# First unit's transposes of probabilities two ticks behind their row instead of one, in a three-branch decoder trunk on one core

## The reference

```
h = rmsnorm(x, norm_g[i]);  proj = h @ w_in[i]
ya = forgetting_attention(qa, ka, va, logf) * silu(za)        # 8 heads of 64, causal, forget-gate bias
yb = nsa_attention(...compressed, selected, window...) * silu(zb)
yc = differential_attention(qc, kc, vc, lam, ...) * silu(zc)  # 4 heads, two maps each
merged = g0*(ya @ w_br_a) + g1*(yb @ w_br_b) + g2*(yc @ w_br_c)
x = x + merged @ w_out[i]
x = x + sigmoid(x @ w_ple_gate[i]) * (p[i] @ w_ple[i])
```

## Time and profile before

| | us |
|---|---|
| median of 3 runs | 1517.42 |
| lowest and highest run | 1516.68, 1519.68 |
| the profiled execution, its own time | 1517.52 |
| its span from the first to the last instruction | 1515.7 |
| TensorE busy | 1476.7 (97%) |
| VectorE busy | 938.1 (62%) |
| ScalarE busy | 634.6 (42%) |
| mean granted clock of TensorE | 0.996 |

### The profile page before, as it was taken

The page is one execution under the profiler, slowest core; times in us unless marked ns, Lnnn a source line. Parts: engine busy times, 40 slices in busy tenths (PEclk is TensorE's granted clock), DMA queues, the critical chain, the costliest instruction groups (busy, mean ns, idle before and its releaser), DMA issues.

```text
span 1515.7 us, 22245 instructions
## 1 busy us (share of the span) xinstructions
PE 1476.7 (97%) x7765; PEld 1225.4 (81%) x7765; DVE 938.1 (62%) x2197; ACT 634.6 (42%) x1499; POOL 75.6 (5%) x79
## 2 busy tenths in 40 slices
PE   7999999999999999999999999999999999999997
PEld 6778778888888887888787887888888888878885
DVE  6866765655557776454576667655556567855544
ACT  6543434434344344343444434334434444434343
POOL 1000000000001000000100000000000000000011
PEclk9999999999999999999999999999999999999998
DMA  7334443223335543332342335423324355433322
GB/s 195 90 82 121 104 112 77 70 70 77 83 93 139 139 119 84 109 102 70 108 110 70 105 99 126 115 54 82 77 63 118 88 131 130 108 102 100 87 87 74
DMA packets 259262, 150.48 MB, mean 99 GB/s; under 512 B 47482, under 2 KB 247764, under 8 KB 259156
## 3 DMA queue, kind: packets, MB, share of 16 engines
q1 hardware_dynamic: 259156, 149.11, 37.8%
HBM read 118.67 MB, written 2.10 MB: 80 GB/s over the span
## 4 chain that ended last, share of the span: by engine, by line
PE 80%; DVE 9%; ACT 3%; issue 3%; DMA 2%; SPq 1%; POOL 0%; ACTq 0%; DVEq 0%; POOLq 0%
PE D L768 21%; PE D L770 20%; PE D L769 20%; PE Ob L959 7%; PE T L937 4%; DVE w_lo L1323 3%; PE S L924 2%; PE S L925 2%; ACT w_hi L1089 1%; DMA arena<-rcs 1%; PE S L914 1%; PE Mb L975 1%; ACT probs L1201 1%; SPq L587 1%; DVE v_b L1418 1%
## 5 line engine op out<-in xcount | busy, mean ns | idle before, releaser
L768 PE MATMUL D<-h_hi,w_hi 128*128 128x512 f32 x1264 | 537.3, 425 | 6.7 <-DVE zs L1473 3.7
L1323 DVE TENSOR_TENSOR w_lo<-raw,w_hi 128x512 fp32r<-128x512 f32 (+2 forms) x504 | 296.7, 628 | 323.3 <-ACT w_hi L1089 323.2
L770 PE MATMUL D<-h_lo,w_hi 128*128 128x512 f32 x1264 | 496.4, 393 | 0.0
L769 PE MATMUL D<-h_hi,w_lo 128*128 128x512 f32 x1264 | 494.4, 391 | 0.0
L1089 ACT ACTIVATE w_hi<-raw 128x512 fp32r<-128x512 f32 (+2 forms) x504 | 263.5, 568 | 290.9 <-PE D L770 288.4
L1201 ACT ACTIVATE probs<-probs,nmax 128x128 f32<-128x128 f32 (+3 forms) x256 | 142.0, 555 | 339.8 <-DVE nmax L1574 339.7
L770 PEld LDWEIGHTS D<-h_lo,w_hi 128*128 128x128 f32 x1264 | 237.4, 188 | 53.1
L768 PEld LDWEIGHTS D<-h_hi,w_hi 128*128 128x128 f32 x1264 | 238.8, 189 | 51.0 <-DVE w_lo L1323 7.5
L769 PEld LDWEIGHTS D<-h_hi,w_lo 128*128 128x128 f32 x1264 | 239.4, 189 | 30.8 <-issue 0.5
L1574 DVE CUSTOM_DVE_ANT_0 probs<-S,maskb 128x128 f32<-128x128 f32 (+3 forms) x256 | 115.1, 487 | 31.2 <-PE S L925 17.4
L552 DVE COPY pT<-T 128x128 f32<-128x128 f32 (+3 forms) x160 | 77.5, 487 | 55.0 <-PE T L937 54.5
(11 more groups left out here) (249 smaller groups left out, 1594.9 us busy)
## 6 DMA issues: line engine op xcount, KB each, us to landing
raw<-in_w_in_dram SPq DMA_DIRECT2D x124, 512.0 KB, 4.0
arena<-rcs SPq DMA_DIRECT2D x48, 256.0 KB, 4.4
raw<-in_w_in_dram SPq DMA_DIRECT2D x32, 256.0 KB, 3.8
arena<-rcs SPq DMA_DIRECT2D x64, 128.0 KB, 2.3
raw<-in_w_out_dram SPq DMA_DIRECT2D x16, 512.0 KB, 4.1
raw<-in_w_ple_gate_dram SPq DMA_DIRECT2D x16, 512.0 KB, 4.2
rcs<-rx SPq DMA_DIRECT2D x80, 64.0 KB, 2.0
raw<-in_cmp_w_k_dram SPq DMA_DIRECT2D x8, 512.0 KB, 3.7
```

Of the source, the lines that this page charges most:

```text
L768: pe.matmul(o, w_hi[:, sl, cs], hi[:, k, :], start=(k == 0), stop=False)
L769: pe.matmul(o, w_lo[:, sl, cs], hi[:, k, :], start=False, stop=False)
L770: ins = pe.matmul(o, w_hi[:, sl, cs], lo[:, k, :], start=False, stop=last)
L1323: TT(w_lo[:, sl, half], raw[:, ring(L, t, RAW), half], f(w_hi[:, sl, half]), ALU.subtract).then_inc(M["dve_lo"], 1)
```

## The change

For unit 0 alone, T of a row is issued when the row's tick lies two ticks back, as it is for branch C; before it was one. V stays one tick behind T. Units 1 to 11 keep their rules.

```diff
--- before.py
+++ after.py
@@ -215,7 +215,7 @@
                 parts.append((("cs", "cx", "ct")[j], s))
             if ti < len(prob_rows):
                 u = prob_rows[ti][0]
-                limit = tick - (2 if branch(u) == "C" else 1)
+                limit = tick - (2 if branch(u) == "C" or u == 0 else 1)
                 while ti < len(prob_rows) and prob_rows[ti][4] <= limit:
                     parts.append(("T", ti))
                     vq.append((tick + (2 if u == UNITS - 1 else 1), ti))
```

## The result

| | before | changed |
|---|---|---|
| median of 22 runs each, us | 1518.70 | 1521.61 |
| lowest and highest | 1516.37, 1521.72 | 1519.66, 1523.55 |
| the profiled execution, its own time | 1517.52 | 1521.02 |
| its span | 1515.7 | 1519.2 |

The change is slower, by about the amount forecast. The interval reaches from 2.1 to 4.1 us, so that both figures are 2.9 is luck in part. The forecast of 1520.3 was set on the 1517.42 of three runs; in this comparison the kernel before took 1518.70, 1.3 more, and the changed one is higher by as much.

A forecast was written before the change was run, and what follows sets the result against it. TensorE, busy 97% of the span, was taken as the bound. ksb0.0 later by 1.9 us in layer 0 and 1.0 in layer 1, all earlier waits included, gave +2.9 on 1517.42: 1520.3 us, range 1517.4 to 1522.4.

The forecast's parts named there:

- The old waits: Unit 0's transposes T4 (both layers) and T0 (layer 1) waiting for exponentials: all 2.48 us go.
- First new wait: V2 in unit 0 waits until VectorE's N0 has read block 0 out of Ob: 1.1 us in each layer.
- Second new wait: VectorE's copy of T10 waits for V8, holding ka2's evacuation: ksb0.0 starts 1.9 us later in layer 0, 1.0 in layer 1.
- VectorE's idle time in front of the copy of T10: Sign in the changed profile: VectorE idle about 3 us before that copy, released by Ob.
- Only the first wait is real: Rival: T10's copy finds V8 done or VectorE catches up, −0.3 us, 1517.1; 9% together with a half-length variant, 1518.7.
- The waits simply go: Rival: N0 and ka2's evacuation are in time, so 2.48 us are gained, 1514.9; 5%.
- A lag of VectorE that is carried on: Rival: unit 1's row maxima, low weights or ksb0's rotation come another 1 us late per layer, 1522.3; 12%.
- The clock: Rival: the wait at ksb0.0 brings the lower clock, 3.2 us more over both layers, 1523.5; 4%.
- The sign "clock 1.00 throughout": Sign in the changed profile: TensorE's granted clock stays at 1.00 throughout.
- The weight loads: No load counted as done during TensorE's waits; if loads reached across, the sum would be 2.8 us.

The follow-up runs named there:

- e1: Changed kernel with T10 and its VectorE copy moved behind V8; 1517.28 us against 1517.14 of the kernel before, ratio 0.9997.
- e2: Kernel before with V8 moved behind the end of ka2, and Y0 and YS0 behind T10; 1521.17 us, ratio 1.0024.
- e3: Kernel before with T0 moved back three dense steps and T4 two, V3 and N1 ahead of T4; 1514.50 us against 1517.14, ratio 0.9980.
- e7: Changed kernel run once more, unaltered, for its profile; 1520.61 us.
- e4: Kernel before with T0, T4 and also unit 1's T12 moved later; 1513.88 us against 1517.14, ratio 0.9974.
- e5: Kernel before with V1 and N0 moved behind ka1.5; 1522.79 us against 1517.07, ratio 1.0038.
- e6: Changed kernel with V8, V9 and N4 moved behind the last step of w1k1; 1524.49 us against 1517.07 of the kernel before, ratio 1.0049.
- e8: Changed kernel run again, unaltered, for a third profile; 1520.84 us.

## Why the prediction was right

*The sum.* Forecast +2.9 us, measured +2.9 by the medians and 2.67 by the two stretches of the trace. The terms were 0.23 too high together and the clock was left out, so the last tenth is luck. The reason held too: e1 takes the second wait out and the loss is gone, e2 puts it alone into the kernel before and the loss is there.

*The old waits, 2.48 us.* Right: e3 takes them away alone and gains 2.6 (1.7 to 4.4 by the interval).

*First new wait.* Forecast 1.1 lost in each layer; measured 0.80 idle, and from 77.64 to 78.84 less the usual 0.23 it is 0.97 lost. It is 0.13 too high: copy, reciprocal and product were taken with the 0.94 us of one place, and took 0.82 here (77.87 to 78.69). Right in mechanism: e1 keeps the wait and comes out even with the kernel before, and 0.3 − 0.6 lies well inside its interval.

*Second new wait.* Forecast 1.9 and 1.0 later at ksb0.0; measured 1.82 and 0.85. VectorE's idle time in front of the copy of T10 was to be about 3 us and was 2.61 in layer 0.

*The rivals.* "Only the first wait is real" is refuted by the 1.75 us of the profile. "The waits simply go" is refuted for the change, and is the result of e3, where only two transposes move. A lag of VectorE that is carried on doesn't show: in e7 the stretch behind ksb0.0 takes as long as before. The clock was given 4%, as a fall behind every such wait; it was seen behind one of the six in three profiles of the changed kernel, at 0.83 instead of 1.6, because T12's wait took up the rest. The sign "clock 1.00 throughout" failed in the first profile. As a rival for the median it fell, but as a term of the sum it was missing: one wait in six at 0.83 is 0.3 us for the two layers. The mean granted clocks of all runs speak for such a term: 0.9965 for the kernel before (30 runs beside e1 to e4), 0.9956 for e2 (11 runs beside them) and 0.9956 for the changed kernel (22 runs, of another time). One fall is about 1.7 us of full clock missing (the parts missing from 1.00 in the windows above), so 0.0009 of 1519 us would be 0.8 falls in an execution, 0.7 us lost, by this estimate. With 2.67 the two figures make 3.0 and 3.3, inside the interval of 2.1 to 4.1. That the clock adds this to the median is argued, not shown; the medians aren't known to so little.

*The weight loads.* The prediction counted no load as done during a wait, by the load before T4. That load may read the probabilities that T4 itself waits for, so it doesn't tell. The load before V2 does, in the changed kernel: its operand pT was copied by 78.29 (77.87 plus 0.42), and it starts at 78.81, beside its matmul at 78.84, which waited for Ob.

## What to carry to other kernels

When an item is moved back in a shared order, look in every engine's queue for what it now stands in front of, and what it waits for there: here a copy of 0.42 us, waiting for a buffer, held an evacuation that the bound engine needed, and cost more than the three waits that were removed. Move only the instruction that waits, by as little as covers its wait (two or three dense steps of 0.7 us here), and not all of its kind by a planner's rule. And a wait of the bound engine is not always priced by its length alone: behind waits near 2 us the clock fell here as well.

## What was not expected of the hardware

The price of a wait of TensorE behind its end. In the profiles of this case, from 60 us on, between dense stretches at a clock of 1.00 (2.4 GHz; 0.50 is 1.2 GHz):

| wait of TensorE, idle us | where | waits | with a fall to 0.50 behind |
|---|---|---|---|
| 2.05 to 2.74 | V2 in e5, ksb0.0 in e6 | 4 | 4 |
| 1.74, 1.75 | ksb0.0 in the changed kernel (three profiles) and e2 | 8 | 2 |
| 0.79 to 0.82 | V2 in the changed kernel (three profiles), e1 and e6 | 10 | 0 |

A fall costs 1.6 us where no other wait follows soon (e5), and 0.82 to 0.84 where T12's wait is behind it and absorbs the rest. It isn't bound to these waits alone: in e8 the clock was 0.50 from 213 to 216 us, behind a wait of only 0.77 and a row of small matmuls (L882), where the profiled execution of the change had the same wait and kept its clock. The same fall stands in e2 in the second layer, from 959 to 961 us:

```profile
957.20 1.08 PE L893 MATMUL Mb<-kcmpT,qf 128*128 128x64 f32 x8 [0.77 <-DVE vbd L1558]
```

These are 2 of the 20 such waits in the ten profiles. Length alone thus doesn't decide, and what else does is open; the counts are small. The start of the program is left out, because the granted clock of the profile can't be relied on there: in the changed kernel's profile it shows 1.00, but the transposes at 10.54 and 11.45 (L752, four matmuls each) take 1.12 and 1.06 us, where those at 10.65 and 11.14 in the kernel before take 0.66 and 0.60.

The Trainium skill (TensorE: Matmul & The Clock Gate, HAM oscillation) warns of waits that throw the engine back to the low clock; its example is a wait of 3 to 5 us for a DMA in every round. The traces agree that a wait can do it, and differ in the length: here it fell behind single waits of 1.74 and 1.75 us, in 2 cases of 8, and of 2.05 us and more, in 4 of 4.
